# 64 unused bytes in front of the transposed scratch of a two-block transformer kernel

## The reference

```python
def first_block(x, ...):                       # DEPTH = 2 layers
    for l in range(DEPTH):
        h = x @ w_in[l]                        # 1024 -> 5024 columns
        q_a = _rms_norm(c_q) @ w_q_up[l]; kv = _rms_norm(c_kv) @ w_kv_up[l]
        y_a = (attention(q_a, k_a, v_a) * silu(gate_a)) @ w_branch_a[l]
        y_b = (_rms_norm(differential_attention(...)) * silu(gate_b)) @ w_branch_b[l]
        merged = g[..., :D] * y_a + g[..., D:] * y_b      # g = sigmoid(gates + b_merge)
        x = _layer_norm(DEEPNORM_ALPHA * x + merged @ w_out[l], ...)

def swiglu(h, wi, wo):
    a, g = jnp.split(h @ wi, 2, axis=-1)       # 1024 -> 2 x 2816
    return (a * jax.nn.silu(g)) @ wo           # 2816 -> 1024

def half_ffn_sublayer(x, mod, j, wi, wo, g, b):
    y = 0.5 * swiglu(modulate(x, mod, j), wi, wo)
    return layer_norm(ALPHA * x + gate * y, g, b)

def second_block(x, c, ctx, ...):
    # layer 0: FFN(x), FFN(ctx), window_sink_attention, FFN(x)
    # layer 1: FFN(x), fourier_mix, FFN(x)
```

## Time and profile before

| | |
|---|---|
| median of 3 runs | 1754.73 us (1753.13, 1754.73, 1819.91) |
| profiled execution, first to last instruction | 1768.5 us |
| TensorE busy (matmuls) | 1664.5 us, 94% |
| VectorE busy | 1230.8 us, 70% |
| ScalarE busy | 810.3 us, 46% |
| mean granted TensorE clock | 0.964 |

### The profile page before, as it was taken

The page is one execution under the profiler, slowest core; times in us unless marked ns, Lnnn a source line. Parts: engine busy times, 40 slices in busy tenths (PEclk is TensorE's granted clock), DMA queues, the critical chain, the costliest instruction groups (busy, mean ns, idle before and its releaser), DMA issues.

```text
span 1768.5 us, 24109 instructions
## 1 busy us (share of the span) xinstructions
PE 1664.5 (94%) x7743; PEld 1346.8 (76%) x7743; DVE 1230.8 (70%) x1947; ACT 810.3 (46%) x1252; POOL 120.0 (7%) x175
## 2 busy tenths in 40 slices
PE   6989889899889999999998998999989998989997
PEld 5877778787778887888875776888868886678876
DVE  6877888778977776777577367777487765375545
ACT  5455445556344444444443245444354443254442
POOL 1100001000011100011000000111001100000000
PEclk9999989999989999999998599999999999999999
DMA  8763549643678874887552005987668873255651
GB/s 316 261 208 120 162 153 321 219 144 116 206 252 262 266 247 139 266 268 253 200 206 95 1 1 167 285 263 260 197 201 266 262 248 133 72 167 189 188 173 67
DMA packets 199330, 345.72 MB, mean 195 GB/s; under 512 B 10852, under 2 KB 127900, under 8 KB 198732
## 3 DMA queue, kind: packets, MB, share of 16 engines
q1 hardware_dynamic: 174668, 252.90, 43.4%
q0 software_dynamic: 24576, 91.73, 16.5%
HBM read 343.54 MB, written 1.05 MB: 195 GB/s over the span
## 4 chain that ended last, share of the span: by engine, by line
PE 84%; DVE 8%; issue 3%; ACT 3%; DMA 2%; SPq 0%; DVEq 0%; POOLq 0%; ACTq 0%
PE acc L513 23%; PE acc L515 23%; PE acc L514 23%; PE score L921 2%; DVE w_lo L1383 2%; PE acc L932 2%; PE score L621 2%; DMA mod_raw<-in_mod_w 1%; PE turn L946 1%; PE turn L831 1%; PE acc L732 1%; PE acc L971 1%; DVE x L1483 1%; PE score L712 1%; ACT turned L1078 1%
## 5 line engine op out<-in xcount | busy, mean ns | idle before, releaser
L1383 DVE TENSOR_TENSOR w_lo<-raw,w_hi 128x1024 fp32r<-128x1024 f32 (+1 forms) x490 | 585.2, 1199 | 307.2 <-ACT w_hi L1014 301.8
L1014 ACT ACTIVATE w_hi<-raw 128x1024 fp32r<-128x1024 f32 (+1 forms) x490 | 507.6, 1041 | 575.3 <-PE acc L515 574.9
L513 PE MATMUL acc<-w_hi,xT_hi 128*128 128x512 f32 (+1 forms) x1456 | 587.3, 403 | 34.2 <-DVE xT_lo L1430 12.4
L514 PE MATMUL acc<-w_lo,xT_hi 128*128 128x512 f32 (+1 forms) x1456 | 573.1, 394 | 0.0
L515 PE MATMUL acc<-w_hi,xT_lo 128*128 128x512 f32 (+1 forms) x1456 | 572.7, 393 | 0.0
L513 PEld LDWEIGHTS acc<-w_hi,xT_hi 128*128 128x128 f32 x1456 | 278.4, 191 | 96.8 <-issue 38.5
L515 PEld LDWEIGHTS acc<-w_hi,xT_lo 128*128 128x128 f32 x1456 | 278.1, 191 | 58.7
L514 PEld LDWEIGHTS acc<-w_lo,xT_hi 128*128 128x128 f32 x1456 | 278.8, 191 | 55.1 <-issue 1.2
L1502 DVE SCALAR_TENSOR_TENSOR acc_lat<-mod_raw,silu_c,acc_lat 128x512 f32<-128x512 f32 x252 | 187.7, 745 | 1.3 <-DMA mod_raw<-in_mod_w 1.3
L513 PE MATMUL acc<-w_hi,hT_hi 128*128 128x512 f32 x440 | 174.9, 397 | 0.7 <-DVE hT_lo L1845 0.2
L514 PE MATMUL acc<-w_lo,hT_hi 128*128 128x512 f32 x440 | 173.8, 395 | 0.0
(11 more groups left out here) (244 smaller groups left out, 1342.8 us busy)
## 6 DMA issues: line engine op xcount, KB each, us to landing
raw<-in_ffn_wi SPq DMA_DIRECT2D x220, 512.0 KB, 5.0
mod_raw<-in_mod_w POOLq DMA_DIRECT2D x144, 512.0 KB, 4.3
raw<-in_ffn_wo SPq DMA_DIRECT2D x110, 512.0 KB, 4.5
raw<-in_w_in SPq DMA_DIRECT2D x72, 512.0 KB, 5.6
raw<-in_w_out SPq DMA_DIRECT2D x16, 512.0 KB, 4.5
raw<-in_attn_wqkv SPq DMA_DIRECT2D x16, 512.0 KB, 4.7
wide<-in_b_merge POOLq DMA_DIRECT2D x4, 1024.0 KB, 9.5
raw<-in_w_branch_a SPq DMA_DIRECT2D x8, 512.0 KB, 4.2
```

What stands on the lines that cost most here:

```text
L513: nc.tensor.matmul(dst, xh, wh, start=start, stop=False)
L514: nc.tensor.matmul(dst, xh, wl, start=False, stop=False)
L1014: nc.scalar.activation(w_hi[:, i % SPLIT_SLOTS, 0:n], raw[:, s, i % 2 * PIECE:i % 2 * PIECE + n], ACT.Copy).then_inc(hi_ready, 1)
L1383: nc.vector.tensor_tensor(w_lo[:, i % SPLIT_SLOTS, 0:n], raw[:, i // 2 % RAW_SLOTS, i % 2 * PIECE:i % 2 * PIECE + n], w_hi[:, i % SPLIT_SL ...
```

## The change

A tensor `pad` of 16 float32 numbers (64 bytes per partition) is allocated between `eps` and `turned`. Nothing reads or writes it. Every tensor that is allocated behind it, in both parts, moves by 64 bytes: those with remainder 64 by 128 get remainder 0. `turned` goes from 136128 to 136192, `hT_hi` from 168896 to 168960, `hT_lo` from 191424 to 191488, `cT_hi` from 221376 to 221440. The small row statistics of both parts move too, by the same 64 bytes. The tensors in front of `pad` stay, among them `raw`, `w_hi`, `w_lo`, `x`, `xT_hi` and `xT_lo`; their addresses have the remainder 128 by 512, `w_hi` for one is at 49280. The instructions of every engine are the same and stand in the same order.

```diff
         mean_factor = sb("mean_factor", [P, 1])
         eps = sb("eps", [P, 1])
+        pad = sb("pad", [P, 16])
         turned = sb("turned", [P, 2, 512])
```

## The result

| | before | after |
|---|---|---|
| median, us (6 runs each) | 1759.71 | 1793.8 |
| lowest and highest, us | 1750.09, 1819.91 | 1788.3, 1815.6 |
| profiled execution: span (its run), us | 1768.5 (1769.74) | 1793.2 (1794.93) |
| granted clock in it, mean | 0.964 | 0.947 |

The ratio is 1.0186, 95% interval 1.0134 to 1.0239: the kernel became slower by 1.9%, or 34 us by the medians, where I forecast 9 us less.

A forecast was written before the change was run, and what follows sets the result against it. TensorE, busy 94% of the span, was taken to bound the kernel and alone pace the second products. Their -8.8 us, all other terms 0, from the 1754.7 us median gave 1745.9, say 1746 us; range 1742 to 1766.

The forecast's parts named there:

- The pace, the term that carried the sum: FFN second products: 1320 matmuls on `hT_hi` and `hT_lo` each start 6.67 ns sooner, -8.8 us.
- If the extra 6.67 ns belong to the remainder of 64, they go: FFN second products: moving to remainder 0 by 128 brings 233.3 ns a matmul to the first product's 226.7.
- the turn against: Rival, FFN second products: a worse distance between stationary and weights' reads costs another 16 cycles, 1763.5 us; chance 0.07.
- nothing changes: Rival, FFN second products: the 16 cycles come from `down` or distance to the weights, not the remainder; 1754.7 us, chance 0.27.
- speak against me: Latents' products on `cT_hi`, `cT_lo`: 16 and 35 cycles above their columns don't fit a plain 16-cycle fee.
- 2.10 means no change: Sign in the second product's timeline: nine steps take 2.04 us if the forecast holds, 2.10 if unchanged, 2.16 if worse.
- The terms at nothing: `cT` products, float32 matmuls, transposes, VectorE, ScalarE, transfers: 0 in the sum; bounds include +1.5 and +-0.6 us.
- the range of the sum: Whole kernel: 1742 to 1766 us, leaving out the clock and a part of the scatter.
- the clock in the attention: Rival, attention: ten more heads at 1.2 GHz add 42.5 us to 1745.9, 1788 us; chance 0.04.
- Nothing in the sum hangs on what made it longer: Profiled execution, 13.8 us above the median: second products lie at full clock, so the same 8.8 us comes off the median.
- the change alters nothing in front of that stretch but the three products' pace: Argument against more attention heads at the low clock: ahead of that stretch only three products' pace changes.

The follow-up runs named there:

- with the clock held: Kernel before and changed kernel, each with 28 unread matmuls added in TensorE's waits ahead of the first attention heads: medians 1752.44 and 1752.1 us.
- att_only: Against the kernel before, only the attention's tensors of the second part moved by 64 bytes: median 1758.2 us, ratio 1.0002; profiled execution 1809.2 us.
- before_plus2: Kernel before with the first matmul of the second product repeated once in each of the first two FFNs: median 1808.53 us, ratio 1.0049.
- all_but_att: The change, with the attention's tensors moved another 64 bytes, back to remainder 64 by 128: median 1806.1 us, ratio 1.0138 to the kernel before.
- after_plus2: Changed kernel with the first matmul of the second product repeated once in each of the first two FFNs: median 1785.35 us, ratio 1.0057 to before.
- after_again: The changed kernel word for word, run again under another label: six runs, median 1807.28 us, 1770.91 to 1814.07.
- before_fill: Kernel before with 28 unread matmuls added in TensorE's waits ahead of the first attention heads: median 1752.44 us, ratio 0.9922.
- the filler: 28 unread matmuls added around the first attention heads; with the 192-byte pad in place of 64 bytes: median 1745.27 us, ratio 0.9899 to the kernel before.

## Why the prediction was wrong

**The pace, the term that carried the sum.** The step that failed was "If the extra 6.67 ns belong to the remainder of 64, they go". They don't belong to it. They belong to the distance between the stationary and the moving operand by 512, which the change moved from 320 to 384, two places of nearly the same price. The term measured 1320 x (233.3 - 232.5) ns = 1.1 us (1.0 us by the five second products) instead of 8.8. That two loops differ by 16 cycles and that their address differs were both read correctly; that the one was the reason was taken for want of another difference, though two rivals had named one: the turn against, and "nothing changes", which had "how far `hT_hi` lies from the weights" among its causes, with 0.27. On the pace that rival was right. Also the stated doubt was right: the `cT` products "speak against me". A fee that three kinds of operand don't share should have cost the remainder more than it did. What would have shown in `down` was right: "2.10 means no change", and it stayed 2.1.

**The rival of the distance**, "it turns against the second product", had the mechanism and the two numbers (320 before, 384 after), and the wrong sign and size: it expected 240 ns and 1763.5 us, and I gave it 0.07. With the distance named, a choice between 0 and 384 was there to be seen: the first product has 0 and is the fast one.

**The terms at nothing.** `cT`, the plain float32 matmuls and transposes, VectorE, ScalarE and the transfers were put at 0. All that isn't clock or second product differs by 0.3 us between the two traces, and with the clock held the kernels are 0.3 us apart in their medians. As a sum these held; inside it the `cT` products got slower by up to 0.3 us, where the prediction saw at most a gain of 0.2. But the range of the sum had no term for the clock, and so ended at 1766. That is the step that put the forecast out: the clock in the attention was put at nothing because "Nothing in the sum hangs on what made it longer", and it measured +21.1 us between the two traces, with +4.3 ahead of the first FFN.

**The clock.** The rival was "the clock in the attention", 1788 us: it was measured at 1793.8. Its place and its price (4.25 us a head) were right; the chance of 0.04 was not. That its sum comes so near is luck. It put ten more low heads on 1745.9, a time taken from the median, where only the profiled execution of 1768.5 us was known to have the six low ones. On the span the sum would be 1768.5 - 8.8 + 42.5 = 1802 us. `att_only`, with all but the end low, has 1809.2. The changed kernel's trace had five more low heads, not ten.

Two things were underrated. One run in three of those shown had 1819.91 us, and the profiled one was 13.8 us above the median, and I called this scatter and took it as equal on both sides. It was the largest term in the kernel, and it isn't noise around a value: it goes in steps, and small edits ahead of it changed how often each step came. "the change alters nothing in front of that stretch but the three products' pace" was the argument against. As little as that suffices: `before_plus2` added 0.44 us to the two second products ahead of the attention in its trace; the change took 0.49 off the same two.

**What caused the 34 us.** Shown: the time is lost at the low clock, above all in the attention (the heads, the segments, the kernels with the clock held). Shown: the attention's addresses aren't needed (`att_only` and `all_but_att`), and no moved address is needed at all (15 of 18 runs with two to twelve added matmuls). Shown in the traces: the head in which the clock rises goes with the place of the attention against the clock's own changes. Consistent, but not settled: that it is the shifted arrival by a few tenths of a microsecond that gives the changed kernel its bad mix. `after_plus2` was to undo it and didn't, and why the bad places come more often stays open. Also the first part of the kernel, ahead of all FFNs, was 4.3 us longer in the profiled execution with 17 us more at the low clock; this too varies between executions of kernels that are alike there (508.70 in `after_again`, and 510.94 in `before_plus2`).

The Trainium skill says of this, in "TensorE: Matmul & The Clock Gate" under What's actually happening, that the gate's monitoring runs freely and is not tied to the kernel's start, so that the same kernel can see its clock rise at different points. That agrees with the ladder of one and the same program, 1749.7 to 1820.9 us over 100 runs. The page adds, for modeling, that the ramp penalty is under 1% of a typical kernel span. That is said of the first rise of the clock; in this kernel it falls again ahead of the attention, and between `before_fill` at 1752.4 and the highest runs lie 3.9%.

## What to carry to other kernels

Before reading a change of a per cent, run the kernel before many times and look whether its times lie in steps; if they do, find the stretch at the low clock, hold the clock there with a few spare matmuls, and compare the two kernels so. Where matmuls of 512 columns follow each other at a slightly different pace in two loops that are alike, compare the distance between the stationary and the moving operand, not either address, and lay the stationary one at the distance that the fast loop has: here `[P, 48]` in place of `[P, 16]`, and the filler, give 1745.3 us. Read the pace of the other shapes after that too, since the 256-column matmuls moved the other way. And a scatter in the runs shown that is larger than the forecast is itself a mechanism, to be priced and given a chance.

## What was unexpected of the hardware

The pace of the fp32r matmuls of 128 x 128 by 512 columns went with the distance of the two operands, and not with either address: means of 227.0, 229.0, 232.5 and 233.3 ns at 0, 448, 384 and 320 by 512. The Trainium skill has, in "SBUF — State Buffer" under A bandwidth-pool intuition that's wrong, a second, independent read port for the loading of weights; no run here shows the ports themselves. The traces do show that the pace depends on how the two operands lie to each other, by up to 6.3 ns of 233.3 in the means. That it is the two reads that meet is the likeliest reading, not a shown one.

A stretch at the low clock can last 130 us while TensorE is busy in nearly all of it (128.22 of 130.00 us in `att_only`). A TensorE that looks full in the profile is no sign of the high clock. And the rise, in all ten traces that have one among the heads, came 0.81 to 0.83 of a head's cycle after a head's start, in a head that a tenth of a microsecond at the attention's start can change for another.
